# Triangular inverses of the delta mixer: from six masked 128x128 levels to 32x32 squares joined by corner blocks

## The chip, the cores and the metric

One NeuronCore of a Trainium2 chip runs the whole kernel. The metric is the device time of one execution in microseconds (us). The names of the engines in the profile are PE (TensorE matmul), PEld (its weight load), DVE (VectorE), ACT (ScalarE), POOL (GpSimd) and SP (SyncE, which issues the weight transfers).

## The reference, cut to what matters

The model is a stack of four blocks over 256 tokens of width 1024. Its first two blocks each begin with a hybrid mixer, and one branch of that mixer is a gated delta rule with 8 heads of 128 keys and 128 values. For each head and chunk of tokens a unit lower triangular system is solved:

```python
decay = jnp.exp(jnp.where(lower, g[..., :, None] - g[..., None, :], -jnp.inf))
kk = jnp.einsum('bnhcd,bnhed->bnhce', k, k)
lmat = jnp.where(strict, beta[..., :, None] * kk * decay, 0.0)
amat = lmat + jnp.eye(DN_CHUNK, dtype=lmat.dtype)
rhs = jnp.concatenate([v * beta[..., None], k * (beta * jnp.exp(g))[..., None]], axis=-1)
sol = lax.linalg.triangular_solve(amat, rhs, left_side=True, lower=True, unit_diagonal=True)
u, w = sol[..., :DV], sol[..., DV:]
```

The rest of the model (projections, stick-breaking attention, dense and expert feed-forward blocks, a state-space layer, a second attention) is the same before and after. All of it is computed in fp32.

## The kernel before, in words

The program is written engine by engine: each engine has one function that lists its instructions in order, and semaphores alone order the engines against each other. `at(name, count, l, total)` and `mixer(name, l)` give the semaphore and the count to wait for in layer `l` (0 or 1). Weights come in 1 MB units through a ring of six buffers, which SyncE fills as TensorE marks units done.

The kernel uses chunks of 128 tokens. There are 16 *chains*, 8 heads by 2 chunks, and each has its own 128x128 matrix; a group of four chains fills one PSUM bank (512 columns of fp32). A layer's `delta(l)` on TensorE (line 560 on) runs:

1. After the projections, prefix sums of the gate and its broadcasts (lines 565 to 568), then 16 products k·k and 16 products q·k (line 579). VectorE scales k·k by beta and decay to `lmat` in slot D (line 1789) and makes the first inverses E, correct in blocks of 2 (lines 1795 and 1796). ScalarE copies q·k to slot A (line 2621).
2. `lmat` is transposed, four chains at a time (line 585), and ScalarE copies the transposes to slot C (line 2624).
3. Six levels double the size of the inverted blocks from 2 to 128. At each level, for four groups of four chains: GpSimd masks the transpose to the off-diagonal blocks of that level (line 2871), TensorE multiplies (line 602), ScalarE copies the product out (line 2629), TensorE transposes the inverse E (line 608), ScalarE copies that to slot F (line 2631); then TensorE multiplies the two (line 620) and VectorE subtracts the product from E (line 1802). Every product is a whole 128x128 matmul. At the last level the operands are swapped, and F receives the transposed inverse.
4. Beside the levels VectorE adds to the exponent of the decay (`u_arg`, line 1804, 2048 columns), multiplies q·k by its exponential (line 1808) and scales q (line 1813); ScalarE does the Exp (line 2634), the third Silu of the convolution (`silus(2)`), the Silu of z and two Sigmoids of the gates (lines 2639 to 2641).
5. `turn(which, n)` transposes eight values or keys (line 627): `turn(2, 0)`, `turn(1, 0)`, `turn(1, 1)` and, once the last level is subtracted, `turn(2, 1)`. VectorE scales each bank of four into slots C and D (`kvt_out`, eight operations). Then come the products with F (lines 672 and 677), VectorE's copy of the first new values (lines 1839 and 1840), the state and the outputs.

The instruction order of each engine is written out by hand in this order; no planner changes it. An fp32 matmul stands in the trace as two records of LDWEIGHTS and MATMUL, a transpose as one.

Lines that only the prediction's comparisons use are these. Line 1101 multiplies with 32x128 weights on four row strips into four banks, and line 1122 with 128x32 weights on four column strips of one bank. Line 1190 has 128x15 weights and 64 moving columns, line 1082 has 32x128 weights and 16 moving columns. Line 2733 is a ScalarE copy of 256 columns. Lines 597 and 615 are waits in the level loop, the first of them at the start of a level's next group and the second ahead of each group of line 620. Line 2360 is ScalarE's rounding of a weight unit, in the projections.

## Time and profile before

| | us |
|---|---|
| median of 3 runs (lowest, highest) | 3185.01 (3184.97, 3190.64) |
| span of the profiled execution | 3187.1 |
| PE busy, share of the span | 3090.6, 97% |
| DVE busy | 2284.0, 72% |
| ACT busy | 1674.9, 53% |
| POOL busy | 112.4, 4% |

Of the profiled execution the span is the only time there is, and it lies within the three runs. A busy share is the time in which an engine had an instruction in work; matmuls overlap, and so a busy PE need not be at its peak. PEclk is the share of TensorE's full clock that was granted in a stretch. In a table of windows each row has the window's ends and its length, the busy time of PE, PEld, DVE, ACT and POOL with their instructions, PEclk, the DMA engines' share and their GB/s. In the chain of waits, each step is led back to what released it, with its start and its length.

### The profile page before, as it was taken

The numbers are of one execution on the slowest core, as the hardware profiler recorded it, in microseconds if no ns is written. First come the engines' busy times: TensorE is split into PE (matmuls) and PEld (weight loads), VectorE is DVE, ScalarE is ACT, GpSimd is POOL, SyncE is SP. The second block draws the span as 40 slices with busy tenths as digits, with TensorE's granted clock in tenths as the row PEclk, the third lists the DMA queues.
The fourth block names the chain that finished last, engine by engine and source line by source line (L and its number), as shares of the span: only waits on it lengthen the run. The fifth ranks groups of instructions, "written<-read, shape, count | busy, mean of one in ns | idle before, by whom it ended". The sixth has DMA issues, their size and how long they took to land.

```text
span 3187.1 us, 50330 instructions
## 1 busy us (share of the span) xinstructions
PE 3090.6 (97%) x21054; PEld 2804.0 (88%) x21054; DVE 2284.0 (72%) x2593; ACT 1674.9 (53%) x1700; POOL 112.4 (4%) x121
## 2 busy tenths in 40 slices
PE   7999999999999999999999999999889999998999
PEld 7999999999999787888888888899779999995899
DVE  7975688847656688888888888688755536447355
ACT  3446443435564677777777777543324414425343
POOL 0004000000040000000000000000000000000000
PEclk8999999989999899999999999999889999998999
DMA  8640388725403499999999999744224544540353
GB/s 353 249 178 1 106 303 305 288 107 184 159 1 110 161 363 367 367 368 364 370 367 365 372 366 363 276 169 180 88 114 178 184 147 169 188 158 13 118 183 123
DMA packets 130026, 703.07 MB, mean 221 GB/s; under 512 B 11184, under 2 KB 15552, under 8 KB 74048
## 3 DMA queue, kind: packets, MB, share of 16 engines
q1 hardware_dynamic: 118816, 650.30, 55.6%
q0 software_dynamic: 6880, 48.24, 3.9%
q8 instruction: 124, 2.03, 0.3%
q10 hardware_dynamic: 4160, 2.12, 0.3%
q14 instruction: 46, 0.38, 0.0%
HBM read 698.50 MB, written 1.07 MB: 219 GB/s over the span
## 4 chain that ended last, share of the span: by engine, by line
PE 90%; DVE 6%; ACT 2%; issue 1%; DMA 1%; POOL 1%; SPq 0%; ACTq 0%; DVEq 0%
PE banks L499 24%; PE banks L500 24%; PE banks L501 24%; PE banks L440 4%; PE banks L620 1%; PE banks L602 1%; PE banks L450 1%; DVE ring_low L1314 1%; DVE big L1314 1%; PE banks L822 1%; PE banks L495 1%; PE banks L608 1%; DMA ring<-in_wall 1%; PE banks L843 1%; POOL tail L2871 1%
## 5 line engine op out<-in xcount | busy, mean ns | idle before, releaser
L1314 DVE TENSOR_TENSOR ring_low<-ring,parts 128x2048 fp32r<-128x2048 f32 x586 | 1335.1, 2287 | 384.4 <-ACT parts L2360 351.9
L499 PE MATMUL banks<-parts 128*128 128x256 f32 (+1 forms) x3968 | 1240.5, 313 | 15.6 <-DVE tail_parts L1314 7.8
L500 PE MATMUL banks<-tail_parts,parts 128*128 128x256 f32 x3744 | 1061.1, 283 | 0.0
L2360 ACT ACTIVATE parts<-ring 128x2048 fp32r<-128x2048 f32 x250 | 479.1, 1916 | 779.0 <-PE banks L501 734.0
L501 PE MATMUL banks<-parts,ring_low 128*128 128x256 f32 x3072 | 869.4, 283 | 0.0
L499 PEld LDWEIGHTS banks<-parts 128*128 128x128 f32 x3968 | 754.2, 190 | 58.0 <-issue 12.4
L2462 ACT ACTIVATE parts<-ring 128x2048 fp32r<-128x2048 f32 x336 | 644.8, 1919 | 215.6 <-DMA ring<-in_wall 211.6
L500 PEld LDWEIGHTS banks<-tail_parts,parts 128*128 128x128 f32 x3744 | 711.1, 190 | 2.0 <-issue 1.9
L501 PEld LDWEIGHTS banks<-parts,ring_low 128*128 128x128 f32 x3072 | 585.3, 191 | 0.0
L501 PE MATMUL banks<-parts,tail_parts 128*128 128x512 f32 x896 | 352.6, 393 | 0.0
L500 PE MATMUL banks<-ring_low,parts 128*128 128x512 f32 x896 | 352.4, 393 | 0.0
L499 PE MATMUL banks<-tail_parts,parts 128*128 128x256 f32 x928 | 262.6, 283 | 0.1
L501 PE MATMUL banks<-tail_parts,ring_low 128*128 128x256 f32 x928 | 262.1, 282 | 0.0
L501 PEld LDWEIGHTS banks<-parts,tail_parts 128*128 128x128 f32 x896 | 168.3, 188 | 40.5
L500 PEld LDWEIGHTS banks<-ring_low,parts 128*128 128x128 f32 x896 | 168.8, 188 | 33.9
L499 PE MATMUL banks<-parts,tail_parts 128*128 128x512 f32 x448 | 177.4, 396 | 1.8 <-DVE tail_parts L1314 1.7
L499 PEld LDWEIGHTS banks<-tail_parts,parts 128*128 128x128 f32 x928 | 176.5, 190 | 0.3 <-issue 0.3
L500 PE MATMUL banks<-ring_low,tail_parts 128*128 128x512 f32 x448 | 176.3, 393 | 0.0
L501 PE MATMUL banks<-parts 128*128 128x512 f32 x448 | 176.3, 393 | 0.0
L501 PEld LDWEIGHTS banks<-tail_parts,ring_low 128*128 128x128 f32 x928 | 176.2, 190 | 0.0
L499 PEld LDWEIGHTS banks<-parts,tail_parts 128*128 128x128 f32 x448 | 84.1, 188 | 23.0 <-issue 3.3
L1314 DVE TENSOR_TENSOR tail_parts<-banks,tail_parts 128x256 fp32r<-128x256 f32 x112 | 47.4, 423 | 79.3 <-ACT tail_parts L2488 78.9
(441 smaller groups left out, 3430.5 us busy)
## 6 DMA issues: line engine op xcount, KB each, us to landing
ring<-in_wall SPq DMA_DIRECT2D x616, 1024.0 KB, 6.6
big<-in_wall POOLq DMA_DIRECT2D x40, 1024.0 KB, 5.7
big<-in_w_k POOLq DMA_DIRECT2D x1, 2048.0 KB, 8.4
big<-in_w_v POOLq DMA_DIRECT2D x1, 2048.0 KB, 13.0
big<-bias_table ACTq DMA_DIRECT2D x2, 1024.0 KB, 8.1
constants<-in_con SPq DMA_DIRECT2D x1, 1249.5 KB, 8.6
x<-in_x SPq DMA_DIRECT2D x1, 1024.0 KB, 7.2
big<-big POOLq DMA_DIRECT2D x16, 64.0 KB, 4.8
```

The lines of the kernel that those rows point to most:

```text
L440: mm = pe.matmul(dst(t), tile(n, k * tiles + t), src[:, src_off + k * width:src_off + (k + 1) * width], start=(k == 0), stop=(k == kt - 1))
L450: mm = pe.matmul(half(b, 0), ones, big(SQ0 + t * TOK, TOK), start=(t == 0), stop=(t == KT - 1))
L495: mm = pe.matmul(o[:, c:c + 1], ada_sum(first + n)[:, t * P:(t + 1) * P], ones[:, 0:1], start=True, stop=True)
L499: pe.matmul(o, high, in_high, start=start, stop=False, **kw)
L500: pe.matmul(o, high, in_low, start=False, stop=False, **kw)
L501: return pe.matmul(o, low, in_high, start=False, stop=stop, **kw)
L602: mm = pe.matmul(bank[q][:, c * P:(c + 1) * P], block(LTS, q, c), block(SLOT["E"], q, c), start=True, stop=True)
L608: mm = pe.transpose(bank[4 + q % 2][:, c * P:(c + 1) * P], block(SLOT["E"], q, c), ident)
L620: mm = pe.matmul(bank[6 + q % 2][:, c * P:(c + 1) * P], inverse_t, u, start=True, stop=True)
L1314: return ve.tensor_tensor(out, a, b, op)
L2360: act(parts(w_high(room, n), UNIT), ring[n % RING][:, :], ACT.Copy).then_inc(sem("w_high"), 1)
L2462: act(parts(slot_at(q), UNIT), ring[r][:, :], ACT.Copy).then_inc(sem("x_high"), 1)
```

## The change

Each 128x128 inverse is now built from its four diagonal 32x32 squares. Slots EC and FC hold the 16 chains' squares compactly: the partitions 32q to 32q+31 hold square q, and each chain takes 32 columns, so that all 64 squares fill 128x512. `square(off, c, q)` is square q of chain c there, and `low_block(c, rows, cols, n)` an n x n block of its `lmat` in slot D. EC holds the inverse and FC its transpose, and both are carried along, so nothing is transposed. Five steps (`SMALL`) take the squares from blocks of 1 to 32. In a step, for two halves g of eight chains, TensorE computes V, VectorE masks it by one 32x32 pattern while it copies it out of PSUM, TensorE computes the updates of F and of T, and VectorE subtracts both. A product of a half is 32 matmuls of 32x32x32 (`tiles`), with square q on row strip q and column strip q of the array and in partitions 32q of one bank. The first step needs V and T only.

Then the squares are joined: V64, F64 and T64 (32x32 blocks) make 64x64 blocks, V128 and F128 (64x64 blocks, `corner`) make the transposed 128x128 inverse in slot F, which GpSimd has set to zero before. ScalarE and VectorE copy and negate between the products. `turn(2, 0)` now waits for the join up to 64 (`f_high`, `t21_a`) and `turn(2, 1)` for both corners.

What else moves: the product of q·k with its exponential and the scaling of q go from VectorE to GpSimd (one 2048-wide, one 1024-wide operation), and VectorE waits for them (`q_decayed`) ahead of its copy of the first new values. ScalarE runs `silus(2)` and the Silu of z first, then waits for `u_arg`, then Exp and the Sigmoids, all ahead of the join's copies. The addition to the exponent is made in two halves of 1024 columns, in steps 1 and 2. In layer 0 ScalarE copies the patterns for the squares out of the constants, during the projections (`block_masks`).

The diff is cut to its core; the lines removed from VectorE and ScalarE are those that the kernel before shows at 1795 to 1813 and 2624 to 2641. The transposes of line 585, the six levels of lines 595 to 621, GpSimd's masks, and the ScalarE copies of lines 2624 to 2631 are gone.

```diff
+        EC, FC, VC32, NEG64 = HB, HB + 512, HB + 1024, HB + 1536
+        NEG128, E64 = SLOT["E"], SLOT["E"] + 1024
+        V_BANK, T_BANK, F_BANK = (4, 7), (5, 0), (6, 1)
+        V64_BANK, F64_BANK, F128_BANK = (2, 3), (4, 0), (6, 7)
+        MASKS = CC["level"] + SMALL * P
+        IDENT32 = MASKS + SMALL * SQ
...
-                for b in range(4):
-                    pe.wait_ge(*at("lmat", b + 1, l, 4))
-                    for c in range(4):
-                        mm = pe.transpose(bank[4 + b][:, c * P:(c + 1) * P], big(SLOT["D"] + (4 * b + c) * P, P), ident)
-                    mm.then_inc(sem("lt"), 1)
...
-                for s in range(6):
-                    for q in range(4):
...
+                def tiles(b, g, lhs, rhs):
+
+                    for c in range(8 * g, 8 * g + 8):
+                        for q in range(4):
+                            mm = pe.matmul(bank[b][SQ * q:SQ * q + SQ, c % 8 * SQ:(c % 8 + 1) * SQ], lhs(c, q), rhs(c, q),
+                                           start=True, stop=True)
+                    return mm
...
+                for s in range(SMALL):
+                    for g in range(2):
                         if s:
-                            pe.wait_ge(*at("level_t", 4 * (s - 1) + q + 1, l, 24))
+                            pe.wait_ge(*at("level_f", 2 * (s - 1) + g + 1, l, 2 * SMALL))
                         else:
-                            pe.wait_ge(*at("level_init", q + 1, l, 4))
-                            pe.wait_ge(*at("qk_out", q + 1, l, 4))
-                        for c in range(4):
-                            mm = pe.matmul(bank[q][:, c * P:(c + 1) * P], block(LTS, q, c), block(SLOT["E"], q, c),
-                                           start=True, stop=True)
-                        mm.then_inc(sem("level_u"), 1)
...
-                        for c in range(4):
-                            mm = pe.transpose(bank[4 + q % 2][:, c * P:(c + 1) * P], block(SLOT["E"], q, c), ident)
-                        mm.then_inc(sem("level_turned"), 1)
...
-                        for c in range(4):
-                            inverse_t, u = block(SLOT["F"], q, c), block(UBUF, q, c)
...
-                            mm = pe.matmul(bank[6 + q % 2][:, c * P:(c + 1) * P], inverse_t, u, start=True, stop=True)
-                        mm.then_inc(sem("level_p"), 1)
+                            pe.wait_ge(sem("block_masks"), 1)
+                            pe.wait_ge(*at("lmat", 2 * g + 2, l, 4))
+                        tiles(V_BANK[g], g, low_of, compact(FC) if s else lambda c, q: ident32(q)).then_inc(sem("level_v"), 1)
...
+                    for g in range(2):
+                        pe.wait_ge(*at("level_vc", 2 * s + g + 1, l, 2 * SMALL))
+                        if s:
+                            pe.wait_ge(*at("level_t", 2 * (s - 1) + g + 1, l, 2 * SMALL))
+                            tiles(F_BANK[g], g, compact(EC), compact(VC32)).then_inc(sem("level_fp"), 1)
+                        elif g:
+                            pe.wait_ge(*at("qk_out", 4, l, 4))
+                        tiles(T_BANK[g], g, compact(VC32), compact(EC) if s else lambda c, q: ident32(q)).then_inc(sem("level_tp"), 1)
...
+                for g in range(2):
+                    pe.wait_ge(*at("level_f", 2 * (SMALL - 1) + g + 1, l, 2 * SMALL))
+                    for c in range(8 * g, 8 * g + 8):
+                        for h in range(2):
+                            mm = pe.matmul(bank[V64_BANK[g]][64 * h:64 * h + SQ, c % 8 * SQ:(c % 8 + 1) * SQ],
+                                           low_block(c, 64 * h + SQ, 64 * h, SQ), square(FC, c, 2 * h + 1), start=True, stop=True)
+                    mm.then_inc(sem("join_p"), 1)
...
+                    pe.wait_ge(*mixer(f"neg64_{ab}1", l))
+                    o = bank[F64_BANK[g]]
+                    for c in range(8 * g, 8 * g + 8):
+                        for h in range(2):
+                            mm = pe.matmul(o[64 * h:64 * h + SQ, c % 8 * SQ:(c % 8 + 1) * SQ], square(EC, c, 2 * h),
+                                           square(NEG64, c, 2 * h), start=True, stop=True)
+                    mm.then_inc(sem("join_p"), 1)
+                    for c in range(8 * g, 8 * g + 8):
+                        mm = pe.matmul(o[SQ:2 * SQ, c % 8 * SQ:(c % 8 + 1) * SQ], square(NEG64, c, 0), square(EC, c, 0),
+                                       start=True, stop=True)
+                    mm.then_inc(sem("join_p"), 1)
+                for g in range(2):
+                    pe.wait_ge(*mixer(f"f_low_{'ab'[g]}", l))
+                    for c in range(8 * g, 8 * g + 8):
+                        mm = pe.matmul(bank[V64_BANK[g]][0:64, c % 8 * 64:(c % 8 + 1) * 64], low_block(c, 64, 0, 64),
+                                       big(SLOT["F"] + c * P + 64, 64, 64, 64), start=True, stop=True)
+                    mm.then_inc(sem("join_p"), 1)
+
...
+                def corner(g):
+
+                    ab = "ab"[g]
+                    pe.wait_ge(*mixer(f"neg128_{ab}", l))
+                    pe.wait_ge(*mixer("e64", l))
+                    pe.wait_ge(*mixer(f"t21_{ab}", l))
+                    for c in range(8 * g, 8 * g + 8):
+                        mm = pe.matmul(bank[F128_BANK[g]][0:64, c % 8 * 64:(c % 8 + 1) * 64], big(E64 + c * 64, 64, 0, 64),
+                                       big(NEG128 + c * 64, 64, 0, 64), start=True, stop=True)
+                    mm.then_inc(sem("join_p"), 1)
...
                 pe.wait_ge(*at("conv_silu", 3, l, 3))
+                pe.wait_ge(*mixer("f_high", l))
+                pe.wait_ge(*mixer("t21_a", l))
                 turn(2, 0)
+                corner(0)
+                corner(1)
                 turn(1, 0)
                 turn(1, 1)
-                pe.wait_ge(*at("level_t", 24, l, 24))
+                pe.wait_ge(*mixer("corner_a", l))
+                pe.wait_ge(*mixer("corner_b", l))
                 turn(2, 1)
...
-                pe.wait_ge(*mixer("q_dec", l))
+                pe.wait_ge(*mixer("q_decayed", l))
...
+                for s in range(SMALL):
+                    for g in range(2):
+                        ve.wait_ge(*at("level_v", 2 * s + g + 1, l, 2 * SMALL))
+                        tt(group(VC32, g), in_bank(V_BANK[g]), const32(MASKS + s * SQ), ALU.mult).then_inc(sem("level_vc"), 1)
+                        if s == 0:
+                            ve.wait_ge(*at("level_vc", g + 1, l, 2 * SMALL))
+                            tt(group(FC, g), const32(IDENT32), group(VC32, g), ALU.subtract).then_inc(sem("level_f"), 1)
...
+                    if s == 1:
+                        ins = ve.scalar_tensor_tensor(chains(SLOT["B"], 8), chains(SLOT["B"], 8), 0.0, each(RS, 0, 8), ALU.min, ALU.add)
+                    elif s == 2:
+                        ve.scalar_tensor_tensor(chains(SLOT["B"] + 1024, 8), chains(SLOT["B"] + 1024, 8), 0.0, each(RS, 0, 8),
                                                 ALU.min, ALU.add).then_inc(mixer("u_arg", l)[0], 1)
-                    elif s == 1:
-                        ve.wait_ge(*mixer("u_exp", l))
-                        tt(big(SLOT["B"], 2048), big(SLOT["A"], 2048), big(SLOT["B"], 2048), ALU.mult)
-                    elif s == 2:
+                    elif s == 3:
                         ve.wait_ge(*mixer("decay_exp", l))
                         tt(SM[:, 144:160], SM[:, 144:160], SM[:, 0:16], ALU.mult)
-                        qv = view(BIG, CONV + P, [[TOK, 8], [1, P]])
-                        tt(qv, qv, view(BIG, EG, [[P, 8], [1, P]]), ALU.mult).then_inc(mixer("q_dec", l)[0], 1)
+                    for g in range(2):
+                        if s:
+                            ve.wait_ge(*at("level_fp", 2 * (s - 1) + g + 1, l, 2 * SMALL - 2))
+                            tt(group(FC, g), group(FC, g), in_bank(F_BANK[g]), ALU.subtract).then_inc(sem("level_f"), 1)
+                        ve.wait_ge(*at("level_tp", 2 * s + g + 1, l, 2 * SMALL))
+                        tt(group(EC, g), group(EC, g) if s else const32(IDENT32), in_bank(T_BANK[g]), ALU.subtract)\
+                            .then_inc(sem("level_t"), 1)
+
...
+                for g in range(2):
+                    ve.wait_ge(*mixer(f"v64_{'ab'[g]}", l))
+                    ve.tensor_scalar(one_block(NEG64, g, 0), bank[V64_BANK[g]][0:SQ, 0:8 * SQ], -1.0, None, ALU.mult)\
+                        .then_inc(sem("join_v"), 1)
+                ve.wait_ge(*mixer("inverse_zero", l))
+                ve.wait_ge(*mixer("e64", l))
+                for g in range(2):
+                    ve.wait_ge(*mixer(f"t64_{'ab'[g]}", l))
+                    ve.tensor_copy(view(BIG, E64 + g * 512, [[64, 8], [1, SQ]], SQ, SQ),
+                                   view(bank[F64_BANK[g]], 0, [[SQ, 8], [1, SQ]], SQ, SQ)).then_inc(sem("join_v"), 1)
+                ve.wait_ge(*mixer("v128_a", l))
+                ve.tensor_scalar(big(NEG128, 512, 0, 64), bank[V64_BANK[0]][0:64, :], -1.0, None, ALU.mult).then_inc(sem("join_v"), 1)
+
+                def corner_out():
+
+                    ve.wait_ge(*mixer("f128_a", l))
+                    ve.tensor_copy(view(BIG, SLOT["F"] + 64, [[P, 8], [1, 64]], 0, 64),
+                                   view(bank[F128_BANK[0]], 0, [[64, 8], [1, 64]], 0, 64)).then_inc(sem("join_v"), 1)
...
+                    if i == 0:
+                        corner_out()
+                ve.wait_ge(*mixer("q_decayed", l))
                 ve.wait_ge(*mixer("vnew_ps", l))
...
+                    if not l and p == 13:
+                        se.wait_ge(sem("con_rest"), CON_PARTS * 16)
+                        for q in range(4):
+                            act(view(CON, MASKS, [[SQ, SMALL], [1, SQ]], SQ * q, SQ),
+                                view(CON, CC["level"] + SQ * q, [[P, SMALL], [1, SQ]], SQ * q, SQ), ACT.Copy)
+                            ins = act(CON[SQ * q:SQ * q + SQ, IDENT32:IDENT32 + SQ], con("ident", SQ, SQ * q, SQ * q, SQ), ACT.Copy)
+                        ins.then_inc(sem("block_masks"), 1)
...
-                for b in range(4):
-                    se.wait_ge(*at("lt", b + 1, l, 4))
-                    act(big(SLOT["C"] + b * 512, 512), bank[4 + b][:, :], ACT.Copy).then_inc(sem("lt_out"), 1)
...
-                        act(big(Z_, 2048), big(Z_, 2048), ACT.Silu)
-                    elif 2 < s < 5:
-                        x = GATES + (s - 3) * 2048
-                        act(big(x, 2048), big(x, 2048), ACT.Sigmoid)
+                silus(2)
+                act(big(Z_, 2048), big(Z_, 2048), ACT.Silu)
+                se.wait_ge(*mixer("u_arg", l))
+                act(big(SLOT["B"], 2048), big(SLOT["B"], 2048), ACT.Exp).then_inc(mixer("u_exp", l)[0], 1)
+                for x in (GATES, GATES + 2048):
+                    act(big(x, 2048), big(x, 2048), ACT.Sigmoid)
...
+                for g in range(2):
+                    ab = "ab"[g]
+                    se.wait_ge(*at("level_f", 2 * (SMALL - 1) + g + 1, l, 2 * SMALL))
+                    diagonal(3, 8 * g, 8)
+                    diagonal(2, 8 * g, 8).then_inc(sem("join_s"), 1)
+                    se.wait_ge(*mixer(f"v64_{ab}", l))
+                    act(view(BIG, NEG64 + g * 8 * SQ, [[1, 8 * SQ]], 64, SQ), bank[V64_BANK[g]][64:64 + SQ, 0:8 * SQ], ACT.Copy, scale=-1.0)\
+                        .then_inc(sem("join_s"), 1)
+                se.wait_ge(*at("level_t", 2 * SMALL, l, 2 * SMALL))
+                for q in range(2):
+                    ins = act(view(BIG, E64 + SQ * q, [[64, 16], [1, SQ]], SQ * q, SQ), view(BIG, EC, [[SQ, 16], [1, SQ]], SQ * q, SQ), ACT.Copy)
...
+                for g in range(2):
+                    se.wait_ge(*mixer(f"f64_{'ab'[g]}", l))
+                    off_diagonal(1, g).then_inc(sem("join_s"), 1)
+                off_diagonal(0, 0)
+                off_diagonal(0, 1).then_inc(sem("join_s"), 1)
+                se.wait_ge(*mixer("v128_b", l))
+                act(big(NEG128 + 512, 512, 0, 64), bank[V64_BANK[1]][0:64, :], ACT.Copy, scale=-1.0).then_inc(sem("join_s"), 1)
+                diagonal(0, 0, 16)
+                diagonal(1, 0, 16).then_inc(sem("join_s"), 1)
+                se.wait_ge(*mixer("f128_b", l))
+                act(view(BIG, SLOT["F"] + 8 * P + 64, [[P, 8], [1, 64]], 0, 64), view(bank[F128_BANK[1]], 0, [[64, 8], [1, 64]], 0, 64), ACT.Copy)\
+                    .then_inc(sem("join_s"), 1)
...
-                for s in range(6):
-                    for q in range(4):
-                        if s:
-                            po.wait_ge(*at("level_u", 4 * (s - 1) + q + 1, l, 24))
-                        else:
-                            po.wait_ge(*at("lt_out", q + 1, l, 4))
-                        po.tensor_tensor(view(BIG, LTS + q * 512, [[P, 4], [1, P]]), view(BIG, SLOT["C"] + q * 512, [[P, 4], [1, P]]),
-                                         view(CON, CC["level"] + (s + 1) * P, [[0, 4], [1, P]]), ALU.mult).then_inc(sem("level_mask"), 1)
+                po.wait_ge(sem("evac"), l * 30 + 36)
+                po.memset(big(E64, 1024), 0.0)
+                po.memset(big(SLOT["F"], 2048), 0.0).then_inc(mixer("inverse_zero", l)[0], 1)
+                po.wait_ge(*mixer("u_exp", l))
+                po.tensor_tensor(big(SLOT["B"], 2048), big(SLOT["A"], 2048), big(SLOT["B"], 2048), ALU.mult)
+                qv = view(BIG, CONV + P, [[TOK, 8], [1, P]])
+                po.tensor_tensor(qv, qv, view(BIG, EG, [[P, 8], [1, P]]), ALU.mult).then_inc(mixer("q_decayed", l)[0], 1)
...
```

## Rows read from the trace of the kernel before

**Rows 1.** Page: the span of the profiled execution.

```profile
span 3187.1 us, 50330 instructions
```

**Rows 2.** Windows: both inversions, then three stretches of small matmuls.

```profile
245.50:304.96 59.46, 57.40 (x498) 55.63 (x497) 29.96 (x34) 41.33 (x61) 36.56 (x24) 1.00 0.01 1
878.70:941.01 62.31, 57.16 (x496) 55.45 (x495) 32.74 (x36) 41.34 (x61) 37.17 (x24) 1.00 0.00 1
2282.00:2285.00 3.00, 3.00 (x57) 2.74 (x60) 2.93 (x4) 0.00 (x0) 0.00 (x0) 0.50 0.00 0
2342.60:2344.50 1.90, 1.90 (x66) 1.70 (x65) 0.00 (x0) 0.00 (x0) 0.00 (x0) 1.00 0.00 0
2352.00:2357.00 5.00, 5.00 (x24) 4.96 (x24) 0.00 (x0) 0.00 (x0) 0.00 (x0) 0.50 0.97 410
```

**Rows 3.** Chain of waits, layer 0 (start us, us, what).

```profile
238.59 7.16 PE banks L579 x64
...
255.90 3.79 PE banks L620 x32
259.69 0.89 PE banks L602 x8
260.58 0.44 PE banks L608 x4
...
305.24 3.49 PE banks L627 x32
...
323.75 0.14 issue
```

**Rows 4.** Chain of waits, the same points of layer 1.

```profile
871.62 7.16 PE banks L579 x64
...
941.29 3.49 PE banks L627 x32
```

**Rows 5.** Chain of waits, matmuls on parts of the array.

```profile
2282.11 3.46 PE banks L1122 x64
2285.57 1.12 PE banks L1101 x32
...
2342.64 1.88 PE banks L1122 x64
...
2346.97 9.94 PE banks L1082 x60
```

**Rows 6.** Lines L1190 and L1122: ns min/median/max, times, shapes.

```profile
L1190 PE MATMUL banks<-parameters,small x8: 217/218/229, 2635.2 to 2635.6; 128*15 128x64 f32 x8
...
L1122 PE MATMUL banks<-big x32: 272/272/296, 2342.6 to 2343.4; 128*32 128x127 f32 x16, 128*32 128x128 f32 x16
```

**Rows 7.** Two waits of TensorE's sequencer (PEldq), around 903.6 us.

```profile
L615 PEldq EVENT_SEMAPHORE  x1: 51/51/51, 903.6 to 903.6; - x1
...
L597 PEldq EVENT_SEMAPHORE  x1: 51/51/51, 903.7 to 903.7; - x1
```

**Rows 8.** Groups by form: busy us, mean ns; GpSimd's L2871 by line.

```profile
L1314 DVE TENSOR_TENSOR tail_parts<-banks,tail_parts 128x256 fp32r<-128x256 f32 x112 | 47.4, 423 | 79.3 <-ACT tail_parts L2488 78.9
L1314 DVE TENSOR_TENSOR big<-big,small 128x1024 f32<-128x1024 f32 x16 | 19.5, 1219 | 0.1
...
L2733 ACT ACTIVATE big<-banks 128x256 f32<-128x256 f32 x8 | 3.2, 402 | 22.4 <-PE banks L1122 22.4
...
L2871 POOL TENSOR_TENSOR tail<-big,constants x48: 1260/1276/3092, 246.9 to 928.0; 128x512 f32<-128x512 f32 x48
```

**Rows 9.** Timeline of layer 0 (start us, us, engine, line).

```profile
265.58 1.91 ACT L2634 ACTIVATE big<-big 128x2048 f32<-128x2048 f32 x1
267.51 1.28 ACT L2570 ACT_TABLE_LOAD   x1
...
305.88 4.87 DVE L1314 TENSOR_TENSOR big<-banks,small 128x512 f32<-128x512 f32 x8
```

**Rows 10.** Waits, 140 to 175 us: us in total, times, longest.

```profile
ACT parts L2360 <- PE banks L501: 16.8, 6, 3.3
```

More of the change, by code:

```diff
@@ L226, in turns, with square, low_block, ident32 @@
             return [(r + f, "cmp", f) for f in range(2 * (i % 2))] + [(r + 2 * (i % 2) + hh, "head", hh) for hh in range(4)]
+        def square(off, c, q):
+            return big(off + c * SQ, SQ, SQ * q, SQ)
+        def low_block(c, rows, cols, n):
+            return big(SLOT["D"] + c * P + cols, n, rows, n)
+        def ident32(q):
+            return CON[SQ * q:SQ * q + SQ, IDENT32:IDENT32 + SQ]
         def big(off, width, p0=0, pn=P):
@@ L596, in delta, with low_of, compact @@
+                def low_of(c, q):
+                    return low_block(c, SQ * q, SQ * q, SQ)
+                def compact(off):
+                    return lambda c, q: square(off, c, q)
+                for s in range(SMALL):
+                    for g in range(2):
                         if s:
-                            pe.wait_ge(*at("level_t", 4 * (s - 1) + q + 1, l, 24))
+                            pe.wait_ge(*at("level_f", 2 * (s - 1) + g + 1, l, 2 * SMALL))
                         else:
-                            pe.wait_ge(*at("level_init", q + 1, l, 4))
@@ L1791, in _, with group @@
                     ins.then_inc(sem("lmat"), 1)
-                ve.wait_ge(*at("lmat", 4, l, 4))
-                for b in range(4):
-                    x = b * 512
-                    lk(tt(chains(SLOT["E"] + x, 4), chains(SLOT["D"] + x, 4), each(CON, CC["level0_lower"], 4), ALU.mult))
-                    tt(chains(SLOT["E"] + x, 4), each(CON, CC["ident"], 4), chains(SLOT["E"] + x, 4), ALU.subtract)\
-                        .then_inc(sem("level_init"), 1)
-                for s in range(6):
-                    for q in range(4):
-                        ve.wait_ge(*at("level_p", 4 * s + q + 1, l, 24))
-                        inverse = big(SLOT["E" if s < 5 else "F"] + q * 512, 512)
-                        tt(inverse, inverse, bank[6 + q % 2][:, :], ALU.subtract).then_inc(sem("level_t"), 1)
-                    if s == 0:
-                        ve.scalar_tensor_tensor(chains(SLOT["B"], 16), chains(SLOT["B"], 16), 0.0, each(RS, 0, 16),
+                def group(off, g):
+                    return view(BIG, off + g * 8 * SQ, [[SQ, 8], [1, SQ]])
@@ new lines, in const32, with in_bank @@
+                def const32(off):
+                    return view(CON, off, [[0, 8], [1, SQ]])
+                def in_bank(b):
+                    return view(bank[b], 0, [[SQ, 8], [1, SQ]])
+                ve.wait_ge(sem("block_masks"), 1)
+                for s in range(SMALL):
[9 more added lines that the diff above has]
+                        ve.scalar_tensor_tensor(chains(SLOT["B"] + 1024, 8), chains(SLOT["B"] + 1024, 8), 0.0, each(RS, 0, 8),
@@ new lines, in one_block @@
+                def one_block(off, g, q):
+                    return view(BIG, off + g * 8 * SQ, [[1, 8 * SQ]], SQ * q, SQ)
+                for g in range(2):
[8 more added lines that the diff above has]
+                                   view(bank[F64_BANK[g]], 0, [[SQ, 8], [1, SQ]], SQ, SQ)).then_inc(sem("join_v"), 1)
@@ new lines, in _, with diagonal @@
+                silus(2)
[4 more added lines that the diff above has]
+                    act(big(x, 2048), big(x, 2048), ACT.Sigmoid)
+                def diagonal(q, first, count):
+                    return act(view(BIG, SLOT["F"] + first * P + SQ * q, [[P, count], [1, SQ]], SQ * q, SQ),
+                               view(BIG, FC + first * SQ, [[SQ, count], [1, SQ]], SQ * q, SQ), ACT.Copy)
@@ new lines, in _ @@
+                se.wait_ge(*mixer("inverse_zero", l))
+                for g in range(2):
+                    ab = "ab"[g]
+                    se.wait_ge(*at("level_f", 2 * (SMALL - 1) + g + 1, l, 2 * SMALL))
[4 more added lines that the diff above has]
+                        .then_inc(sem("join_s"), 1)
@@ new lines, in _ @@
+                for g in range(2):
+                    se.wait_ge(*mixer(f"f64_{'ab'[g]}", l))
[6 more added lines that the diff above has]
+                diagonal(1, 0, 16).then_inc(sem("join_s"), 1)
```

43 lines of the change are left out of this document (15 added, 28 removed).

## The prediction

> **What bounds the kernel now.** The page gives the span that this sum is made against [rows 1]; it is 2.1 us above the median of the three runs (3185.01), so I sum changes against 3187.1 and take 2.1 off at the end. A difference under 0.2% (6 us) is what a measurement of this kernel can't tell from none.
>
> The stretches of the two inversions come next [rows 2]. TensorE is busy for 57.4 of 59.5 us in layer 0 and 57.2 of 62.3 us in layer 1, at its upper clock level (granted 1.00, 2.4 GHz), while VectorE and ScalarE have idle time and the DMA share is 0.01 or less: the weight ring is full. So TensorE sets the time here, and what it saves is not needed by a transfer.
>
> The chain of waits says what TensorE does [rows 3]. A level is four blocks of L602 (0.89 us each) and of L608 (0.44) and then L620 (3.79): 9.11 us, six times. From the end of the q·k products (238.59 + 7.16 = 245.75) to the start of the last of the four turns (L627: 305.24 + 3/4 of 3.49 = 307.86) it is 62.1 us in layer 0. In layer 1 [rows 4] the same two points are 878.78 and 943.91: 65.1 us, because the first masks on GpSimd come later. These 127.2 us are what the change rebuilds; all else in it is moved beside them.
>
> **What a small product costs.** One fp32 matmul is two records (weight load and matmul each); a transpose is one. Now 96 + 96 matmuls and 96 transposes per layer; after it 128 matmuls in the first step, 192 in each of the next four (896, or 1792 records) and 112 to join. No row has a 32x32x32 matmul, so I bound it.
> - L1122 puts 128x32 weights on four column strips: 64 records in 1.88 us at the upper clock, 29 ns each, while L620 on the whole array takes 3.79/32 = 118 ns. Four strips do run beside each other (4 x 29 = 117). L1101, with four row strips, shows it too: 32 records in 1.12 us, 35 ns [rows 5].
> - A record of 64 columns lasts 218 ns, one of 128 lasts 272 [rows 6]: 0.84 ns a column. With 32 columns a strip's 117 ns become 117 - 81 = 36, and with four diagonal squares in turn a record is 9 ns. I take 9. The lower end is streaming alone, 32 x 0.84 / 4 = 7 ns; the upper end is 29 to 35 ns, no gain from the narrow tile.
> - The sequencer must keep up. Between the wait at L615 (903.6) and that at L597 (903.7) it passed eight weight loads and eight matmuls of L620 [rows 7], so 0.2 us at most for 16 instructions even with rounding, under 13 ns each, and likelier half of that.
>
> **The step after the change.** A block of 32 matmuls is 64 x 9 ns = 0.58 us. A step has six: V of both halves, then F and T of each, 3.46 us. Between V and F stands one VectorE operation on 128x256 out of PSUM, 0.42 us [rows 8], a matmul's latency (218 - 54 + 27 = 0.19) and two handovers (0.14, the issue gap before L707 in rows 3). Of these 0.9 us the other half's V hides 0.58, so a step is 3.8 us. VectorE's own six operations, 2.5 us, fit. The two additions to the exponent (1024 wide, 1.22 us) stand between VectorE's V and F work in steps 1 and 2; there they wait beside TensorE's F block and cost some 0.3 us in all. First step: four blocks and VectorE's extra subtraction, 2.9 us. Last inverse square: 2.9 + 3 x 3.8 + 3.95 + 0.3 = 18.55 us after the q·k products.
>
> **The join.** ScalarE's queue leads: two diagonal copies and a negation of the second half (3 x 0.40, L2733's size), two E64 copies (512 wide, 0.6 each), one off-diagonal copy 0.4, handovers 0.3: 3.1 us. Then TensorE: V128 twice (16 records of 64 columns on one strip, 117 - 54 = 63 ns, 1.0 us each), a turn 0.87, two corners 2.0, two turns 1.75. Sum 9.7, and the last turn starts 28.25 us after the q·k products. Gain 62.1 - 28.25 = 33.9 and 65.1 - 28.25 = 36.9: 70.7 us.
>
> **Given back.** VectorE's corner copy stands in the row of eight turn copies (4.87 us [rows 9], 0.61 each) which leads the next product: 0.5 per layer. While ScalarE leads the join, TensorE issues little; if its clock falls, V128, corners and turns (7.6 us) double. I take 3 of these 7.6 per layer; both ends, 0 and 7.6, go to the range. Together 7.
>
> **Moved at no cost.** GpSimd loses 24 masks and gets one 2048-wide and one 1024-wide product. At 1.26 to 3.09 us for 512 columns [rows 8] they take 7.5 to 18.6 us. They start after u_arg (step 2, about 256), the Exp and, new here, a table load (1.28 + 1.91 [rows 9]), so near 259, and end at 267 to 278. VectorE now waits for them before it copies the first new values, at about 277.5, with all later VectorE work behind that wait: covered, but for 0.5 at the worst. ScalarE's Sigmoids end near 264, when the first diagonal copies are wanted: even. The memsets (GpSimd idle) lie 15 us before use. Layer 0's copying of masks on ScalarE, eight small operations, falls into gaps of up to 3.3 us in which it waits for TensorE [rows 10]; uncovered it would be 3 us once.
>
> **Sum.** 3187.1 - 70.7 + 7 = 3123.4; less 2.1: **3121 us**.
>
> **Rivals.**
> - **A, the forecast**, 58%.
> - **B, the clock falls in the levels too.** For: L1082 has 32-row weights and 16 columns, and TensorE issued 60 such records without a gap from 2346.97 on [rows 5]; yet from 2352 to 2357, busy for 5.00 of 5.00 us, it was granted 0.50, the lower level of 1.2 GHz [rows 2]. The new stage also uses a quarter of the array. Against: 32 columns on four squares stream most of the time, not a tenth of it. At 1.2 GHz (granted 0.50 around 2282 [rows 2]) L1122 takes 3.46/64 = 54 ns [rows 5], so 4 x 54 - 96 x 1.68 = 55 per strip, 14 a record: block 0.9, step 5.7, levels 26.9, join 16.6, together 43.5. Gain 18.6 + 21.6 less 6 for warming up: 34, so 3151. 22%.
> - **C, the squares take turns**, as all four write one bank. L1122 writes one bank, but from one row strip; L1101 uses four row strips, but four banks: neither shows both. Then 27 ns a record: 48.4 + 0.5 + 10.5 = 59.4 us, gain 2.7 + 5.7, so 3177. 7%. The Trainium skill ("TensorEngine Tiling (Array Packing)", "Gotcha 1: PSUM Pressure") says that different row tiles can't use the same PSUM bank simultaneously; by that rule C would be what happens. No row here shows it.
> - **D, the issue binds, and it is slower.** A record costs its issue, whatever its width. L1101's 35 ns is the nearest price: 1792 x 35 = 62.7, + 0.5 + 11.3 = 74.5, a loss of 12.4 + 9.4, so 3207. It decides from (62.1 - 11)/1792 = 29 ns a record on. Against: L1122's 29 ns, and rows 7. 9%. The Trainium skill ("Runtime: NRT & Kernel Launch", "Instruction fetch mechanics") gives an issue floor of some 20 cycles an instruction; at the 1.2 GHz of the sequencer that is an estimate of 33 ns a record and 3200 us. L1122's rate is already below it.
> - The rest, 4%: that a wait behind the join or on GpSimd's products takes the gain.
>
> **The numbers.** Likeliest is A, 3121. Range: A at 7 ns a record, with the step then bound by its waits (0.8 less each, four steps, two layers) and no fall of the clock (6) is 3108; B with its own error of some 9 is 3160. A and B within it hold 78%. Faster: A, B, half of C, a little of the rest: 0.85; same: the other half of C and rest, 0.06; slower: D, 0.09.
>
> **What would show it.** Right: some 1800 records of the small products per layer at 7 to 12 ns, steps of 3.8 us, granted clock 1.00 in the levels, last turn 28 us after the q·k products, stages after it unchanged. Wrong: records of 27 ns or more (C, D), clock 0.50 in the levels (B), or VectorE waiting for GpSimd before the new values.

## The result and the profile after

The changed kernel takes 3194.43 us, the kernel before 3187.80 (medians of 17 runs each); the ratio is 1.0018, with a 95% interval of 1.0012 to 1.0025. It is slower by a little under 0.2%, where 3121 was forecast. The page of the profiled execution after and its row for the fetched instructions (queue: packets, MB, share of 16 engines):

```profile
span 3192.6 us, 56260 instructions
...
q8 instruction: 147, 2.41, 0.3%
```

The span is 5.5 us longer than before [rows 1]. The same row of the page before has 124 packets, so the change fetches 23 packets more for 56260 - 50330 = 5930 more instructions: some 258 instructions a packet of 16 KB.

The chain of waits after (start us, us, what), first layer 0, then the same points of layer 1. L603 is the q·k products, L610 the small products, L641 to L656 the joins to 64, L662 V128, L673 the corners, L681 the turns:

```profile
238.29 7.14 PE banks L603 x64
245.43 1.13 PE banks L610 x89
...
250.35 1.80 PE banks L610 x128
252.15 1.93 issue
254.07 1.93 PE banks L610 x97
256.00 1.90 issue
257.90 1.93 PE banks L610 x95
...
299.53 3.60 PE banks L662 x32
303.13 1.90 PE banks L681 x8
305.03 3.60 PE banks L673 x32
308.63 4.43 PE banks L681 x24
...
882.52 1.93 PE banks L610 x142
...
946.16 4.80 PE banks L681 x24
```

From the end of the q·k products to the end of the last turn it is 308.63 + 4.43 - 245.43 = 67.6 us in layer 0 and 946.16 + 4.80 - 882.52 = 68.4 in layer 1. Before it was 305.24 + 3.49 - 245.75 = 63.0 [rows 3] and 941.29 + 3.49 - 878.78 = 66.0 [rows 4]. That is 4.6 + 2.4 = 7 us lost, against 5.5 of the span: nothing else in the kernel moved much. By the forecast's steps the two distances would have been 32.6 us (18.55 + 9.7, one turn of 0.87 and 3.5 given back).

The rows show a pattern that the forecast doesn't have: bursts of 1.93 us, then 1.5 to 2.1 us in which TensorE waits for nothing that the profile knows ("issue"). A whole burst is 128 matmul records and as many weight loads, 256 instructions, which is one packet (a row of the chain counts at times fewer records than ran, x97 or x95). The levels' 1792 matmul records are 14 such bursts, and 14 x 3.5 us are the 48.9 us of the levels. The waits of 243 to 325 us (total, times, longest) put numbers on it, and the windows (columns as in rows 2) show the clock as well:

```profile
PE banks L610 <- issue: 22.9, 14, 2.1
```

```profile
245.43:294.31 48.88, 25.97 (x1801) 24.09 (x1802) 14.34 (x32) 14.60 (x11) 6.83 (x2) 0.55 0.02 4
294.31:308.63 14.32, 13.77 (x244) 13.05 (x232) 4.73 (x9) 5.96 (x13) 0.00 (x0) 0.50 0.02 3
```

TensorE has work for 26 of 48.9 us, no other engine for more than 15, and the clock is at the lower level (0.50, 1.2 GHz) from about 250 us on and through the join. The view of the transfers of 245 to 305 us says what comes in meanwhile, after and, below it, before:

```profile
q8 instruction: 15, 0.25, 1.7%
```

```profile
q8 instruction: 4, 0.07, 0.6%
```

In the transfers of 250 to 260 us, packets start near 251.3, 255.3 and 259.1, each 1.0 to 1.4 us after a burst has begun (250.35, 254.07, 257.90), and the next burst begins some 2.7 us after the packet. From these three it looks like one block on its way at a time, ordered when the block before it begins to run.

### The profile page after: what moved, and what is told of

Same layout as the page of the kernel before. It is cut to its first block, busy times and chain, and to the rows that moved or that the text cites. A ratio compares the mean times of both kernels' runs of the same rounds, so it can differ in the third digit from the quotient of the medians.

```text
span 3192.6 us, 56260 instructions
## 1 busy us (share of the span) xinstructions
PE 3055.5 (96%) x24094; PEld 2766.5 (87%) x24094; DVE 2255.9 (71%) x2599; ACT 1639.7 (51%) x1638; POOL 57.8 (2%) x81
## 4 chain that ended last, share of the span: by engine, by line
PE 88%; DVE 6%; issue 3%; ACT 2%; DMA 2%; SPq 0%; ACTq 0%; DVEq 0%
PE banks L523 24%; PE banks L524 23%; PE banks L525 23%; PE banks L464 4%; DMA ring<-in_wall 2%; PE banks L610 2%; PE banks L474 1%; DVE ring_low L1373 1%; DVE big L1373 1%; PE banks L519 1%; PE banks L881 1%; PE banks L902 1%; DVE tail L1373 0%; ACT parts L2454 0%; DVE big L1690 0%
## 5 line engine op out<-in xcount | busy, mean ns | idle before, releaser
L525 PEld LDWEIGHTS banks<-parts,tail_parts 128*128 128x128 f32 x896 | 168.3, 188 | 40.6
L1373 DVE TENSOR_TENSOR tail<-tail,banks 128x256 f32<-128x256 f32 (+1 forms) x180 | 84.6, 470 | 65.8 <-PE banks L610 40.2
```

The source lines that it names most:

```text
L525: return pe.matmul(o, low, in_high, start=False, stop=stop, **kw)
L1373: return ve.tensor_tensor(out, a, b, op)
```

## The experiments

Theory **F** is that reading: TensorE gets its instructions in blocks of 256, one every 3.5 us. Its rivals are C and D of the prediction, under which a record costs 27 ns by itself (48.9 us / 1792). Theory **K** came later: what is left when F's cost is gone is the lower clock.

**Fewer fetches, same products (roll, roll5).** The steps are alike but for the counts that they wait for, so `roll` makes steps 2 to 5 a loop on TensorE. The waits that depend on the turn sit on four products of one column (`after`):

```diff
-                for s in range(SMALL):
+                def after(b, *waits):
+
+                    for name, value in waits:
+                        pe.wait_ge(sem(name), value)
+                    pe.matmul(bank[b][0:64, 511:512], con("ident", 64, 0, 0, SQ), con("ident", 1, 0, 0, SQ), start=True, stop=True)
+
+                def step(s):
...
                     for g in range(2):
...
-                        tiles(V_BANK[g], g, low_of, compact(FC) if s else lambda c, q: ident32(q)).then_inc(sem("level_v"), 1)
+                        after(V_BANK[g], ("level_f", s * 2 + (base + g - 1)))
+                        tiles(V_BANK[g], g, low_of, compact(FC)).then_inc(sem("level_v"), 1)
...
+                with pe.Fori(1, SMALL) as s:
+                    step(s)
...
```

> Steps 2 to 5 of the squares become one loop on TensorE that is run four times; the same products run in the same order, with four one-column products a step more to carry the waits. Theory F (instructions arrive in blocks of 256, one about every 3.5 us, and TensorE waits for them): only the first turn of the loop has to be fetched (3 blocks, 10.5 us, after 2 blocks or 7 us for the first step); the other three go at the array's own speed, 3.9 us at the upper clock to 5.8 us at the lower. Levels 29 to 35 us instead of 48.9, fetches of instructions in the stretch down from 14 to 5 or 6, whole kernel 3154 to 3166. Rivals C (the four squares take turns) and D (a record costs 27 ns to issue): nothing that they charge for is changed, 3194 within 6.

`roll5` puts the first step in as well: VectorE sets FC and GpSimd EC to the identity, and the loop is `pe.Fori(0, SMALL)`.

> The first step goes into the loop too (inverse and transpose start as the identity, written by VectorE and GpSimd), so the loop runs five times. F: 3 blocks, 10.5 us, for the first turn and then four turns of 3.9 to 5.8 us: levels 26 to 34 us, whole kernel 3149 to 3164. C and D: 64 products a layer more, 128 records of 27 ns, 3.5 us a layer: about 3201.

Measured: `roll` 3162.54 us, ratio to before 0.9916 (0.9899 to 0.9932); `roll5` 3155.63, 0.9889 (0.9872 to 0.9906). F holds, C and D fall: `roll` runs the same records in the same order 32 us cheaper, with the loop's code fetched once, and `roll5`, with 128 records a layer more, is 39 us cheaper. Both times lie in F's ranges. The chain of `roll`, the end of the first turn of the loop and the second turn (L624 is a carrier):

```profile
253.29 1.54 PE banks L610 x103
254.82 1.55 issue
256.37 0.58 PE banks L610 x25
256.95 0.30 PE banks L624 x2
257.25 1.53 PE banks L610 x100
258.78 1.24 issue
260.02 0.64 PE banks L610 x28
260.66 0.31 PE banks L624 x2
260.97 1.01 PE banks L610 x64
...
263.58 1.86 PE banks L610 x128
...
267.69 0.36 PE banks L624 x2
```

The gaps end with the first turn. From the second on there is none of that size, a turn is 267.69 - 260.66 = 7.0 us, and a record takes 1.86 / 128 = 14.5 to 1.01 / 64 = 15.8 ns at the lower clock. The levels take 37 us instead of the 29 to 35 expected, as I had not counted the carriers (4 x 0.30 us a turn). In `roll5` the page counts 126 packets of instructions, 21 fewer than in the changed kernel, and 5 instead of 15 of them come in 245 to 305 us.

**Columns against instructions (wide, halves).** `wide` streams the columns of each product but every eighth twice, `halves` makes two products of each:

```diff
-                            mm = pe.matmul(bank[b][SQ * q:SQ * q + SQ, c % 8 * SQ:(c % 8 + 1) * SQ], lhs(c, q), rhs(c, q),
-                                           start=True, stop=True)
+                            n = 1 + (c % 8 < 7)
+                            o, x = c % 8 * SQ, rhs(c, q)
+                            o = bank[b][SQ * q:SQ * q + SQ, o:o + n * SQ]
+                            if n == 2:
+                                x = bass.AP(tensor=x.tensor, offset=x.offset, ap=[list(x.ap[0]), [0, 2], [1, SQ]])
+                            mm = pe.matmul(o, lhs(c, q), x, start=True, stop=True)
```

```diff
-                            mm = pe.matmul(bank[b][SQ * q:SQ * q + SQ, c % 8 * SQ:(c % 8 + 1) * SQ], lhs(c, q), rhs(c, q),
-                                           start=True, stop=True)
+                            for x in (0, 16):
+                                o = c % 8 * SQ + x
+                                mm = pe.matmul(bank[b][SQ * q:SQ * q + SQ, o:o + 16], lhs(c, q), rhs(c, q)[:, x:x + 16],
+                                               start=True, stop=True)
```

> Each small product but every eighth streams its 32 columns twice, into 64 columns of which the next product overwrites the second half: the same number of instructions, almost twice the columns. F: bursts of 3.4 us instead of 1.93 at the lower clock that fill the 1.6 to 1.9 us in which TensorE waited, levels 49 to 53 us, kernel 3189 to 3203. D: no change, 3194. C (turns on the bank, so that columns set the time): 27 ns a record become 50, 42 us a layer more, 3278.

> Each small product is made in two halves of 16 columns: the same columns, twice the instructions. F: 28 blocks instead of 14 at 3.5 us, 49 us a layer more, 3292. D: 1792 records more a layer at 27 ns, 48 us a layer, 3291. C, if columns alone set the time: no change, 3194.

Measured: `wide` 3193.23, 1.0016 (1.0005 to 1.0026), level with the changed kernel; `halves` 3297.59, 1.0340 (1.0319 to 1.0361), 103.2 us more than the changed kernel for 175 - 147 = 28 more packets: 3.7 us each. Nearly twice the columns cost nothing, twice the instructions cost the whole stage again. Of `halves`, the page's row, and of `wide`, a window in the levels and two rows of its chain (L615 are its small products):

```profile
q8 instruction: 175, 2.87, 0.3%
```

```profile
250.00:270.00 20.00, 10.06 (x685) 9.26 (x689) 6.41 (x13) 4.55 (x4) 0.35 (x1) 1.00 0.02 4
```

```profile
253.88 1.89 PE banks L615 x119
255.77 1.94 issue
```

How `wide` did it was not as expected: its bursts did not get longer. The clock was granted 1.00 instead, with TensorE busy for only 10.06 of 20 us, and a burst took 1.89 us, nearly twice the columns at twice the clock. So in the levels as they are unrolled the clock is worth nothing: the fetch sets the time at either.

**The lower clock (roll5w, roll5h, roll5wf, widef, roll5hf).** The first two are `roll5` with the edit of `wide`, for seven chains of eight and for every other one (`c % 2 == 0`). The three with an f have, in the join, four products that nobody reads behind V64 and behind each half's F64 and T64:

```diff
+                def fill(n):
+                    for _ in range(n):
+                        pe.matmul(bank[1][:, 0:P], ident, ident, start=True, stop=True)
+                fill(4)
...
                     mm.then_inc(sem("join_p"), 1)
+                    fill(4)
```

> The loop of five turns, with each small product but every eighth streaming its 32 columns twice. In the loop alone a step took 7.07 us at granted 0.50, all of it TensorE's products (14.5 to 15.7 ns a record) and the carriers of the waits (4 x 0.30 us). Theory K (what is left over the forecast is the lower clock, and the clock stays up when the products stream more columns, as it did where only the columns were doubled): granted 1.00 in the levels, 15.7 ns a record, step 6.0 + 0.6 = 6.6 us, levels 2 us a layer shorter; if the clock stays up in the join too, 5 us a layer less there: 3142 (3150 if the join falls to 0.50). Rival (the clock goes by the share of the array in use, a quarter in both): granted 0.50, 28 ns a record, step 12 us, 25 us a layer more, 3205.

> The loop of five turns, with every other small product streaming its 32 columns twice (48 columns in the mean). K: granted 1.00, 11.8 ns a record, step 4.5 + 0.6 = 5.1 us, levels 10 us a layer shorter: 3135, or 3125 with the join at the upper clock. If 48 columns do not keep the clock up: 20 ns a record at 0.50, step 8.9 us, 9 us a layer more, 3175.

> As the loop with doubled columns, and four products of 128x128x128 that nobody reads in each of three places of the join at which TensorE waits for ScalarE. K: granted 1.00 through the join, its products and turns at half their time there, 5 us a layer less than without them where the join had fallen to 0.50, no change where it had not. Rival: the added products only stand in the way, 12 x 2 records of 118 ns, up to 2.8 us a layer more.

> The changed kernel, unrolled as it is, with the doubled columns and with four products of 128x128x128 that nobody reads in each of three places of the join. It asks what the lower clock alone costs the change as it stands. K: the join and the turns go at granted 1.00; V128, corners and turns take 7.8 us as in the loop with the same products, not 13.8 us; 6 us a layer less, 1 us a layer more for the added products and their 48 instructions: 3183 to 3185. If the clock does not hold through the join: 3194 to 3197. Either way far from the 3121 forecast, since F keeps 14 blocks of instructions a layer in the levels.

> The loop of five turns with 48 columns in the mean and the added products of the join. If the clock holds in the first turn, levels 33 us and join 13 us: 3151. If it dips there as it did without the added products (254 to 260 us at 0.50), 2 us a layer more: 3155, no better than the loop alone.

Measured: `roll5w` 3161.62, 0.9917 (0.9901 to 0.9934); `roll5h` 3160.38, 0.9914 (0.9897 to 0.9930); `roll5wf` 3157.86, 0.9907 (0.9891 to 0.9924); `widef` 3197.36, 1.0030 (1.0017 to 1.0042); `roll5hf` 3155.86, 0.9902 (0.9888 to 0.9916). Their windows say what the clock did. First `roll5w`, then `roll5wf`:

```profile
260.00:280.00 20.00, 19.75 (x1222) 18.95 (x1210) 10.14 (x21) 8.12 (x8) 6.85 (x2) 1.00 0.00 0
280.00:295.00 15.00, 14.42 (x187) 13.64 (x184) 5.41 (x10) 7.34 (x14) 0.00 (x0) 0.58 0.01 2
```

```profile
260.00:280.00 20.00, 19.62 (x1212) 18.76 (x1205) 9.71 (x20) 7.73 (x6) 6.85 (x2) 1.00 0.00 1
280.00:295.00 15.00, 15.00 (x349) 14.05 (x336) 7.23 (x14) 7.83 (x15) 0.00 (x0) 1.00 0.01 2
```

As K has it, the doubled columns kept the clock at 1.00 in the levels, the join of `roll5w` fell to 0.58, and the added products held it at 1.00 in `roll5wf`. In `roll5wf` V128, the first turn, the corners and the other turns are these rows:

```profile
287.27 2.00 PE banks L678 x32
289.28 1.02 PE banks L697 x8
290.30 2.00 PE banks L689 x32
292.31 2.77 PE banks L697 x24
```

They take 2.00 + 1.02 + 2.00 + 2.77 = 7.8 us instead of 3.60 + 1.90 + 3.60 + 4.43 = 13.5. But no time came of it that can be told from `roll5`, and K's times for `roll5w` (3142 or 3150) and `roll5h` (3135 or 3125) were missed. What was added to the products takes back much of what the clock gives: a turn of `roll5wf` takes 6.56 us (261.25 to 267.81), against 7.07 at the lower clock in layer 0 of `roll5`. And in layer 1 `roll5` itself was granted 0.86 in the mean (865.5 to 902.0), so that it had less to gain: there a turn with nothing added took 4.93 us (881.64 to 886.57). In layer 0 of `roll5h` and `roll5hf` the clock dipped to 0.50 at 255 to 260, behind the first turn with its waits for code; `roll5hf` then took the time that its expectation has for that case (3155). In `widef`, with those waits in every step, the added products did not hold it: 0.50 at 305 to 315 again, as the second branch of its expectation has it.

**The step of the forecast (roll5p, roll5q).** Here the carriers keep the array busy: whole-array products, one or two a wait, 32 columns again, `fill` kept.

```diff
-                    pe.matmul(bank[b][0:64, 511:512], con("ident", 64, 0, 0, SQ), con("ident", 1, 0, 0, SQ), start=True, stop=True)
+                    for _ in range(1):
+                        pe.matmul(bank[b][:, 384:512], ident, ident, start=True, stop=True)
```

> The loop of five turns with 32 columns a product again; the four carriers of the waits in a step are now products of 128x128x128 that use the whole array (one each, nobody reads them), and the join has its added products. It asks for the step of the forecast: fetched code, upper clock, 32 columns. If the carriers keep the clock up: 8.3 ns a record, 3.2 us a step, + 4 x 0.24 = 4.2 us and a few waits for VectorE; levels 10.5 + 4 x 4.3 = 28 us, last turn 41 us after the q.k products instead of 48.5 in the loop with 48 columns: 3141. If the clock falls all the same: step 7.5 us, 3160.

> The same with two such carriers for each wait. If one was too few for the clock and two are enough: step 3.2 + 8 x 0.24 = 5.1 us, last turn 45 us after the q.k products: 3148. If one was enough: 1 us a step more than with one, 8 us in all more, 3149.

Measured: `roll5p` 3153.71, 0.9890 (0.9873 to 0.9906); `roll5q` (`range(2)`) 3161.82, 0.9922 (0.9905 to 0.9938). One turn of `roll5p` (L625 is a carrier; of the blocks of 64 and 128 records the chain counts 50 and 83, the others are in the trace too, 392 records in this turn):

```profile
263.50 0.48 PE banks L625 x2
263.99 0.68 PE banks L610 x50
264.67 0.42 PE banks L625 x2
265.09 0.68 PE banks L610 x50
265.77 0.42 PE banks L625 x2
266.19 1.24 PE banks L610 x83
267.43 0.42 PE banks L625 x2
267.85 1.24 PE banks L610 x83
269.09 0.21 issue
269.30 0.48 PE banks L625 x2
```

At the upper clock and with its code at hand, a record takes 1.24 / 128 = 9.7 to 0.68 / 64 = 10.6 ns. The turn is 5.8 us, of which the carriers are 1.74 (0.42 to 0.48 each, not the 0.24 expected); without them it is 4.06, where the forecast has 3.8. The upper-clock turn of `roll5` in layer 1 gives the same, 4.93 less 0.87 of carriers. That both missed (3141 and 3148) lies in these carriers and in the first two turns, in which the clock dipped again (0.50 at 255 to 260 in both).

**A wait that cost nothing (roll5e).** In the fourth turn of `roll5p` the chain ran through a 16-column VectorE product that took 2.00 us. `roll5e` moves it to step 1:

```diff
-                    elif s == 3:
+                    if s == 0:
                         ve.wait_ge(*mixer("decay_exp", l))
                         tt(SM[:, 144:160], SM[:, 144:160], SM[:, 0:16], ALU.mult)
```

> The loop with one carrier of 128x128x128 a wait, and VectorE's 16-column product moved from step 4, where it lies beside GpSimd's 2048-wide product, to step 1, before that product starts. There it took 2.00 us, from 271.96 to 273.96, and ended with GpSimd's product (269.40 + 4.53 = 273.93); in the changed kernel, where GpSimd had gone on to its next product, 0.17. If it is held up by GpSimd's product: 0.17 us in step 1, the wait of 3.4 us in the fourth turn (271.59 to 274.96) goes down to the 0.3 of the other turns, 3 us a layer less: 3148. If it is slow for another reason: it is slow in step 1 too, 3154.

Measured: 3155.23, 0.9898 (0.9881 to 0.9914), level with `roll5p`. The product took 0.17 us in its new place, so GpSimd had held it up, but the turn went from 5.81 us (269.30 to 275.11) to 5.79 (268.13 to 273.92): TensorE had products to run meanwhile. The chain had named VectorE for a stretch in which TensorE was as late.

## Why the prediction was wrong, point by point

- **The small products.** Right: 9 ns forecast, 9.7 to 10.6 measured at the upper clock, 14 (case B) against 14.5 to 15.8 at the lower. Case C is out. The Trainium skill's rule behind it ("TensorEngine Tiling (Array Packing)", "Gotcha 1: PSUM Pressure") finds no support here: four row strips wrote one bank at these rates.
- **"The sequencer must keep up."** This is the step that failed. Its row [rows 7] shows how fast 16 instructions that are already there are passed on, and it was used for whether thousands can be had. The fetch asks 3.5 us for 256, 13.7 ns an instruction or 27 ns a record (a weight load and a matmul), three times the 9 ns taken, and no wait for another engine could hide it. In the kernel before, a level of 80 matmul records and as many weight loads took 9.11 us [rows 3], so a block lasted 14.6 us and its fetch was covered.
- **The step and the levels.** 18.55 us forecast, 48.9 measured in both layers (245.43 to 294.31, 882.52 to 931.41); the missing 30.3 us a layer are the fetch and the clock together. With the fetch gone and the lower clock kept (`roll5`, layer 0) a turn is 7.07 us, 5.9 without the carriers, against the 5.7 of case B; at the upper clock 4.06 against 3.8. The model of the step was right, and what fed it was not in it.
- **The clock (B).** It did fall, and not only in the join. In the unrolled levels that is worth nothing (`wide`); in the join it is 13.5 - 7.8 = 5.7 us a layer, where 3 of a possible 7.6 were taken. B's own 3151 is near what `roll5` shows (3155.63), in part by luck: `roll5` also pays for its carriers and the fetches of its first turn, and had the upper clock for most of layer 1's loop.
- **The join.** 9.7 us, one turn and the 3.5 given back make 14.1; measured 18.8 in layer 0 (294.31 to 313.06). The clock accounts for 5.7 instead of 3; most of the rest is the part ahead of V128, 5.2 us instead of 3.1 (294.31 to 299.53). The forecast has ScalarE lead it and puts nothing for TensorE there; in the chain it is TensorE's own products up to 64 (L641 to L656) at the lower clock, with a gap of 0.55 us for code in it.
- **D** had the side and nearly the size, 35 ns a record against 27, for another reason: it charges each record its issue, and `roll` issues the same records at half that. Its break-even of 29 ns lies above the 27 measured; the longer join made up the difference. The Trainium skill ("Runtime: NRT & Kernel Launch", "Instruction fetch mechanics") has the block of 256 instructions, fetched while another runs; the packets agree (258 instructions each). That the issue floor hides the fetch is where the traces differ: the gap is 1.5 to 2.1 us a block. Nor did the loop's jump back force a fetch, which that section expects of a jump out of its window of two such blocks: a turn is 768 instructions in its products alone, and behind the first turn of `roll` a turn begins within 0.1 us.
- **Moved work.** Right: GpSimd's two products took 4.53 and 2.33 us, less than the lower bound of 7.5, and in 243 to 325 us VectorE has no wait for GpSimd.

The best versions here, `roll5p` at 0.9890, `roll5` at 0.9889 and `roll5e` at 0.9898, can't be told apart and beat both kernels by about 1%. The forecast's 3121 would need, at the least, the first turn's 3 blocks fetched ahead and the upper clock without carriers or added products; neither was tried.

## What to carry to other kernels

Before cutting a product into many small ones, count the instructions of the straight-line code and divide by the time that they are to run in: here a block of 256 per 3.5 us was what TensorE got. A short pause in which an engine waits for nothing, repeated after the same number of instructions, was the sign here, and a loop over code that was already there took it away. A rate measured on a dozen instructions holds for a dozen.

## What the runs showed of the hardware that was not expected

The clock did not follow the busy share. `wide` was granted 1.00 with TensorE busy for 10.06 of 20 us (the window above), and `roll5`, with half the columns a product, 0.50 with TensorE busy all the time, as this window of its loop shows:

```profile
255.00:260.00 5.00, 5.00 (x297) 4.76 (x290) 2.73 (x5) 0.00 (x0) 0.00 (x0) 0.50 0.00 0
```

Nor did it go by the columns alone. In layer 1 of the same run the same loop was granted 0.50 from 875 to 880 and 1.00 from 885 to 900, with TensorE about as busy (4.79 of 5.00 us from 885 to 890); the same block of 128 records in two turns, one behind the other:

```profile
877.54 1.86 PE banks L610 x128
...
883.67 1.24 PE banks L610 x83
```

Why the clock came back in layer 1 and not in layer 0 was not tested and stays open.

VectorE's 16-column product of two operands in SBUF was held for as long as GpSimd's ran. The timeline of `roll5p` (start us, us, engine, line):

```profile
269.40 4.53 POOL L3010 TENSOR_TENSOR big<-big 128x2048 f32<-128x2048 f32 x1 [39.68 <-ACT big L2740]
270.51 0.42 DVE L1386 TENSOR_TENSOR tail<-banks,constants 128x256 f32<-128x256 f32 x1 [0.96 <-PE banks L610]
271.96 2.00 DVE L1386 TENSOR_TENSOR small<-small 128x16 f32<-128x16 f32 x1
```

It ends at 273.96, GpSimd's at 273.93; out of GpSimd's way it takes 0.17 us (`roll5e`, in step 1), and an operation that reads PSUM keeps its 0.42 beside GpSimd's. The 0.17 us of the changed kernel are no case of the two beside each other, as the expectation of `roll5e` takes them: they stand at 277.19, and GpSimd's second product had ended by 276.43. The Trainium skill ("SBUF — State Buffer", "SBUF: two separate sides") says that a VectorE operation with two SBUF inputs and a GpSimd operation that reads SBUF exclude each other for a whole instruction; these rows agree. The change brought this about by moving a product to GpSimd; in `roll5p` it cost nothing because TensorE was as late. In layer 1 of `roll5`, where the product was held for 2.88 us at the upper clock, its turn took 5.48 us (886.57 to 892.05) instead of the 4.93 of the turn before.
